# The residual x turned by VectorE in 32x32 blocks and kept in DRAM, instead of by TensorE in the out projection

## The chip, the cores and the metric

The kernel runs on one core of a Trainium2 chip. The metric is device time in microseconds, the median of several executions. TensorE (PE) multiplies, VectorE (DVE), ScalarE (ACT) and GpSimd (POOL) work elementwise, and SyncE (SP) issues most of the DMAs; each engine runs its own instructions in order, and semaphores tie them together.

## The reference

One decoder layer for 1024 prompt rows and 32 sample rows (8 sequences of 4), T = 1056 rows of D = 1024, all in fp32. Cut to what matters:

```python
def hybrid_layer(x, p, ...):
    h = rmsnorm(x, norm_mix)
    proj = h @ w_in                       # q, k, v, decay and beta, z, short conv b, c, h
    qkv = silu(causal_dwconv(qkv_in, w_conv_qkv))
    o, s_new = gated_delta_rule(q, k, v, log_a, beta, s0)   # 4 heads x 128, in chunks
    o = rmsnorm(o, w_gdn_norm) * silu(z)
    y_sc = B * causal_dwconv(C * h)       # the short convolution mixer
    x = x + concatenate([o, y_sc]) @ w_out    # the out projection, and its residual
    u = relu(rmsnorm(x, norm_mlp) @ w_up)
    x = x + (u * u) @ w_down
    x = x + sigmoid(rmsnorm(x, norm_ple) @ w_ple_gate) * (p @ w_ple_proj)
    return x, ...                          # then a last rmsnorm; conv rows and states are outputs too
```

## The kernel before, in words

Everything is kept transposed: features on the 128 partitions, the 1056 rows along the free axis, in three thirds of 352 (`TH`), one PSUM bank (`pg0` to `pg2`) each. Every product of fp32 numbers is made of three, from high and low parts: w_hi with act_hi, w_hi with act_lo, w_lo with act_hi. The work on TensorE is a row of units of 128 output features: a unit is 3 thirds of 24 matmuls (8 blocks of 128 input features, three products each).

For each unit SP loads 512 KB of weights into one of two buffers (`load_w`), ScalarE makes w_hi of them when TensorE has ended the unit before last (`split_w`, its line shows as L1164), VectorE makes w_lo (L1569), and only then may TensorE begin. VectorE takes each third out of PSUM; TensorE may begin third n of a unit when third n of the unit before is out (`group`, the wait on `evacuated`).

The order of stages: x is loaded in rows and turned by TensorE (L753), with a small product for the decays. Units 1 to 4 are k, 5 to 8 q (L695), 9 to 12 v, then z and the short convolution. During units 1 to 8 VectorE takes out the thirds (L1626, L1628), makes w_lo of the unit after next, then runs the causal convolution of the unit (L1646, L1649) and, in some units, a short chain of small operations for the decays; ScalarE makes SiLU of it. From unit 9 on, TensorE's matmuls are dealt out between the steps of the delta rule by a plan written out by hand (`ORDER`): a step name, chunk, level, and the number of matmuls of the units (L813) that follow. The plan's step `begin` on SP writes the decays as rows to DRAM (L589), waits until they have landed, reads them back twice (L570) and then loads the weights of units 10 and 11.

The out projection is 8 units (`out_unit`). The first takes the mix as soon as its parts are made (L1063), the low parts by VectorE (L1917) and POOL (L2310). The residual x is loaded from the input by SP, a block of 128 features of all rows at a time, into `x_col` (`load_xcol`); behind each third of products TensorE turns the matching pieces (3, 4 and 4 of them, L1041) into the banks `bk0` to `bk2`; ScalarE copies each third to `xres`, and VectorE adds the products (L2014). ScalarE squares each third for the next norm and POOL sums the squares. In the last unit ScalarE and VectorE also split each third of all of x into act_hi and act_lo (L2001) for the MLP, whose first unit waits for them third by third, with the sums of squares (L1075) behind its second third.

Of the kernel before, what the change touches and what calls it, by code (L numbers as in the profile page):

```python
# [105 lines left out]
class Signals:  # L106


    def __init__(self, sem):
# [71 lines left out]
        self.xcol_turned = sem("xcol_turned")  # L181
        self.xcol_turned3 = sem("xcol_turned3")
        self.xr_copied = sem("xr_copied")
# [60 lines left out]
def trunk(nc, x_p, x_s, st_qkv, st_gdn, st_sc, p_p, p_s, norm_mix, w_in, w_cq, a_log, dt_bias, w_gn, w_cs,  # L244
# [8 lines left out]
    g_dram = nc.dram_tensor("g_rows", (NTT * H, P), f32, kind="Internal").ap()  # L253
    y_dram = nc.dram_tensor("ysc_spill", (NSC * P, T), f32, kind="Internal").ap()
# [9 lines left out]
    with ctx:  # L264
# [31 lines left out]
        stage_x.close()  # L296
        qkv = sb("qkv", [P, NQ, T], scope=mixer)
# [69 lines left out]
        late = ExitStack()  # L367

        qkv_room = sb("qkv_room", [P, NQ, T], scope=late)
        x_col = [sb(f"x_col{i}", [P, NTT + 1, P], scope=late) for i in range(2)]  # L370
        late.close()
# [18 lines left out]
        xcol_in = [sem(f"xcol_in{i}") for i in range(2)]  # L390
        y_sent = [sem(f"y_sent{i}") for i in range(3)]
# [3 lines left out]


# [125 lines left out]
        def _(sp):  # L522
# [41 lines left out]
            for b in range(U_QKV + 2, U_V + 1):  # L564
                load_in(b)
# [6 lines left out]
            def load_xcol(x, i):  # L572
                f = ds(i * WIDE + x * P, P)
                sp.dma_start(x_col[x][:, 0:NTT, :], x_p[0].rearrange("(t p) d -> p t d", p=P)[:, :, f]) \
                    .then_inc(xcol_in[x], 16)
                sp.dma_start(x_col[x][0:TS, NTT, :], x_s.rearrange("b t d -> (b t) d")[:, f]) \
                    .then_inc(xcol_in[x], 16)
# [8 lines left out]
            for k, c, l, a, e in PLAN:  # L586
# [52 lines left out]
                if k == "sum" and c == NTT - 1:  # L639
                    load_y(1, slice(TP - 2 * P, T), NTT)  # L640
                    sp.wait_ge(sm.s_updated, 4 * NTT)
                    sp.dma_start(os_p[0, 0].rearrange("h d e -> d h e"), S[:, :, :]).then_inc(sm.states_out, 16)
                    for x in range(2):
                        load_xcol(x, 0)
# [7 lines left out]
            with sp.Fori(1, KD // 2) as i:  # L652
                for x in range(2):
                    load_w(U_OUT + x, i, wout_v[:, :, ds(i * WIDE + x * P, P)], KD)
                    sp.wait_ge(sm.xcol_turned, at(x - 1, i, 2))
                    load_xcol(x, i)
# [32 lines left out]
        def _(pe):  # L689
# [337 lines left out]
            for i in range(NSC):  # L1027
# [4 lines left out]
            pieces = [[(0, 0, 128, 0), (1, 0, 128, 128), (2, 0, 96, 256)],  # L1032
                      [(2, 96, 128, 0), (3, 0, 128, 32), (4, 0, 128, 160), (5, 0, 64, 288)],
                      [(5, 64, 128, 0), (6, 0, 128, 64), (7, 0, 128, 192), (8, 0, 32, 320)]]

            def turn_residual(x, i, n):

                pe.wait_ge(sm.consts_made, 3)
                pe.wait_ge(xcol_in[x], at(32, i, 32))
                for t, a, e, c in pieces[n]:  # L1040
                    last = turn(bk[n][:, c:c + e - a], x_col[x][a:e, t, :], ident[a:e, a:e])  # L1041
                last.then_inc(sm.xcol_turned if n == 2 else sm.xcol_turned3, 1)
# [11 lines left out]
            for n in range(3):  # L1054
# [11 lines left out]
                turn_residual(0, 0, n)  # L1066
# [95 lines left out]
        def _(act):  # L1162
# [59 lines left out]
            def silu_unit(b):  # L1222

                act.wait_ge(sm.conv_step, 4 * b)
# [194 lines left out]
            def out_pair(i):  # L1419
                last = isinstance(i, int)  # L1420
                for x in range(2):
                    b = U_OUT + x
                    def residual(n):

                        act.wait_ge(sm.xcol_turned if n == 2 else sm.xcol_turned3,
                                    at(x + 1, i, 2) if n == 2 else at(2 * x + n + 1, i, 4))
# [968 lines left out]
```

## Time and profile before

| | us |
|---|---|
| median of 3 runs | 1544.12 (1543.38 to 1544.9) |
| the profiled execution | 1544.85 |
| its span | 1542.9 |
| PE busy | 1496.4 (97%), 9412 matmuls |
| DVE busy | 726.8 (47%) |
| ACT busy | 483.8 (31%) |
| POOL busy | 248.5 (16%) |

Times in the rows are counted from the start of the span. "Busy" of PE is a modelled end of each matmul: one of 352 columns shows as 0.32 us while the next starts 0.16 us after it, so the pace is read from the starts. In a row of the timeline "x3" are three instructions merged; in brackets stands how long the engine sat idle before it, and what ended that. "issue" means that nothing in the profile shows what it waited for, which is often a DMA. The span's stages: x turned to 30 us, k and q units to 129, the mixer to 534, the out projection to 645, MLP to 1400, then the gated embedding and the last norm.

### The profile page before, as it was taken

The page shows a single profiled execution, that of the slowest core. Times are in us where ns is not written, and L with a number is a line of the kernel's source. Part 1 is how long each engine was busy: PE and PEld are TensorE (multiplying, and loading weights), DVE is VectorE, ACT ScalarE, POOL GpSimd, SP SyncE. Part 2 cuts the span into 40 slices and gives each one's busy share as a digit, 9 for nine tenths or more (in the row PEclk, how much of TensorE's full clock was granted, in tenths as well). Part 3 has the DMA queues.
Part 4 walks back from the last instruction along what each step waited for, and adds up shares of the span by engine and source line. Part 5 has one row for each costly group of instructions (what it writes and reads, how often), then busy time and mean ns, then how long its engine had stood idle before and what let it go on. Part 6 is the DMA issues. An engine that isn't in the chain of part 4 may idle for free.

```text
span 1542.9 us, 24976 instructions
## 1 busy us (share of the span) xinstructions
PE 1496.4 (97%) x9412; PEld 1458.7 (95%) x9412; DVE 726.8 (47%) x1305; ACT 483.8 (31%) x878; POOL 248.5 (16%) x306
## 2 busy tenths in 40 slices
PE   7998899899999999999999999999999999998997
PEld 6998898799999989899999999999999999998997
DVE  5666943377685632443433333333433433335525
ACT  6223432223333432543212131221302213136525
POOL 3200312043544542200000000000000000040303
PEclk9999997799999999999999999999999999999998
DMA  7212312312122223111111111111111111112102
GB/s 173 56 28 68 84 32 65 116 28 70 36 76 87 81 71 83 55 56 41 42 55 41 41 55 41 41 55 41 41 55 41 45 51 41 49 47 61 36 28 113
DMA packets 140204, 89.82 MB, mean 58 GB/s; under 512 B 16204, under 2 KB 134156, under 8 KB 140119
## 3 DMA queue, kind: packets, MB, share of 16 engines
q1 hardware_dynamic: 139110, 84.89, 19.2%
q0 software_dynamic: 1008, 3.79, 0.6%
q8 instruction: 55, 0.90, 0.3%
q14 instruction: 31, 0.25, 0.1%
HBM read 77.97 MB, written 10.69 MB: 57 GB/s over the span
## 4 chain that ended last, share of the span: by engine, by line
PE 89%; DVE 4%; issue 2%; POOL 2%; ACT 1%; DMA 0%; DVEq 0%; POOLq 0%; ACTq 0%; SPq 0%
PE pg L695 65%; PE pg L813 13%; PE bk L870 1%; DVE act_lo L2001 1%; PE bk L884 1%; PE bk L888 1%; PE bk L1041 1%; PE bk L840 1%; PE bk L1021 1%; POOL act_lo L2310 1%; PE bk L921 0%; DVE cv L1649 0%; PE bk L854 0%; PE bk L901 0%; PE bk L933 0%
## 5 line engine op out<-in xcount | busy, mean ns | idle before, releaser
L695 PE MATMUL pg<-act_hi,w_hi 128*128 128x352 f32 x1344 | 437.9, 326 | 12.5 <-issue 4.8
L695 PE MATMUL pg<-act_lo,w_hi 128*128 128x352 f32 x1344 | 431.8, 321 | 0.0
L695 PE MATMUL pg<-act_hi,w_lo 128*128 128x352 f32 x1320 | 423.2, 321 | 0.0
L695 PEld LDWEIGHTS pg<-act_hi,w_hi 128*128 128x128 f32 x1344 | 252.9, 188 | 16.4 <-issue 8.8
L695 PEld LDWEIGHTS pg<-act_lo,w_hi 128*128 128x128 f32 x1344 | 253.5, 189 | 0.0
L695 PE MATMUL pg<-u_hi,w_hi 128*128 128x352 f32 x768 | 249.3, 325 | 0.0
L695 PE MATMUL pg<-u_hi,w_lo 128*128 128x352 f32 x768 | 248.9, 324 | 0.0
L695 PE MATMUL pg<-u_lo,w_hi 128*128 128x352 f32 x768 | 247.8, 323 | 0.0
L695 PEld LDWEIGHTS pg<-act_hi,w_lo 128*128 128x128 f32 x1320 | 247.5, 188 | 0.0
L2351 POOL TENSOR_TENSOR ssq<-ssq,sq 128x352 f32<-128x352 f32 x72 | 78.1, 1098 | 892.4 <-ACT sq L1164 891.5
L1164 ACT ACTIVATE w_hi<-w_raw 128x1024 fp32r<-128x1024 f32 x111 | 117.1, 1055 | 333.8 <-PE pg L695 303.9
L2048 DVE TENSOR_TENSOR xres<-xres,pg 128x352 f32 (+1 forms) x192 | 99.2, 520 | 200.9 <-PE pg L695 200.9
L1569 DVE TENSOR_TENSOR w_lo<-w_raw,w_hi 128x1024 fp32r<-128x1024 f32 x110 | 141.9, 1290 | 69.0 <-ACT w_hi L1164 68.9
L813 PE MATMUL pg<-act_hi,w_hi 128*128 128x352 f32 x480 | 162.7, 339 | 2.9 <-DVE pre L1626 2.3
L813 PE MATMUL pg<-act_hi,w_lo 128*128 128x352 f32 x480 | 162.2, 338 | 0.0
L813 PE MATMUL pg<-act_lo,w_hi 128*128 128x352 f32 x480 | 160.4, 334 | 0.0
L695 PEld LDWEIGHTS pg<-u_hi,w_hi 128*128 128x128 f32 x768 | 145.0, 189 | 0.0
L695 PEld LDWEIGHTS pg<-u_lo,w_hi 128*128 128x128 f32 x768 | 144.5, 188 | 0.0
L695 PEld LDWEIGHTS pg<-u_hi,w_lo 128*128 128x128 f32 x768 | 143.9, 187 | 0.0
L1164 ACT ACTIVATE sq<-tm 128x352 f32<-128x352 f32 x96 | 48.0, 500 | 230.7 <-DVE tm L2034 230.7
L2038 DVE TENSOR_TENSOR u_lo<-sq,u_hi 128x352 f32 x96 | 50.5, 526 | 130.3 <-ACT u_hi L1164 130.3
L813 PEld LDWEIGHTS pg<-act_hi,w_hi 128*128 128x128 f32 x480 | 93.2, 194 | 8.8 <-issue 5.9
(333 smaller groups left out, 1685.3 us busy)
## 6 DMA issues: line engine op xcount, KB each, us to landing
w_raw<-in_w_up SPq DMA_DIRECT2D x32, 512.0 KB, 4.0
w_raw<-in_w_down SPq DMA_DIRECT2D x32, 512.0 KB, 3.4
w_raw<-in_w_in SPq DMA_DIRECT2D x29, 512.0 KB, 4.4
x_tok<-in_x_prompt SPq DMA_DIRECT2D x8, 512.0 KB, 7.3
w_raw<-in_w_out SPq DMA_DIRECT2D x8, 512.0 KB, 4.9
x_col<-in_x_prompt SPq DMA_DIRECT2D x8, 512.0 KB, 3.7
w_raw<-in_w_ple_gate SPq DMA_DIRECT2D x8, 512.0 KB, 4.0
out<-y_tok SPq DMA_DIRECT2D x8, 512.0 KB, 2.7
```

The lines of the kernel that those rows point to most:

```text
L695: last = mm(pg[bank][:, 0:TH], w, a, start=i == 0, stop=i == len(terms) - 1)
L813: last = mm(pg[n][:, 0:TH], w, (act_hi, act_lo, act_hi)[r][:, k, cols(n)], start=k == 0 and r == 0, stop=k == KD - 1 and r == 2)
L840: last = mm(bk[4][:, c:c + 8], S_in[:, h, i, :], F0[:, c:c + 8], start=True, stop=True)
L870: per_head(lambda h, v: mm(A[x][:, v], LY[x][:, h, :], X[x][:, h, :], start=True, stop=True)) \
L884: last = per_head(lambda h, v: mm(A[x][:, v], XT[s][x][:, h, :], LY[x][:, h, :], start=True, stop=True))
L888: last = per_head(lambda h, v: mm(bank[:, v], LY[x][:, h, :], XT[s][x][:, h, :], start=True, stop=True))
L1021: mm(bk[c % 4][:, :], F0[0:TS, c // 2 * P:(c // 2 + 1) * P], by_seq[c % 4][0:TS, :, :], start=True, stop=True).then_inc(sm.q_pe, 1)
L1164: return nc.scalar.activation(out, in_, func, **kw)
L1569: tt(w_lo[b % 2][:, :, :], w_raw[b % 2][:, :, :], w_hi[b % 2][:, :, :].bitcast(f32), SUB) \
L2038: tt(rows(u_lo[c % 2][:, k, cols(n)]), sq[g % 2][:, :], rows(u_hi[c % 2][:, k, cols(n)]).bitcast(f32), SUB).then_inc(sm.u_lo_made, 1)
L2048: tt(x_t, x_t, pg[g % 3][:, 0:TH], ADD).then_inc(sm.evacuated, 2)
L2351: tt(ssq[:, cols(n)], ssq[:, cols(n)], sq[g % 2][:, :], ADD).then_inc(sm.ssq_added, 1)
```

## The change

x for the residual is turned during units 1 to 8 and kept in DRAM in the transposed layout (`x_turned_rows`, 1024 x 1056). For each block j of 128 features SP loads x so that a partition holds a row of every 32 rows' block: four DMAs of 32 partitions (256 rows each, runs of 512 bytes). One VectorE instruction transposes all 32x32 blocks of a 128x1024 tile, and four DMAs store it in runs of 1 KB, which puts the blocks in their places. The 32 sample rows of all blocks go in one tile, with runs of 128 bytes both ways. The first loads wait until x has been squared, since their buffers lie over its room (and over that of q, k and v, not yet made).

VectorE does blocks 0, 1 and the samples behind unit 1's convolution, block j behind unit j's for 2 to 7. SP stores each and loads the block two further on, between its loads of weights; ScalarE waits for the last stores before SiLU of unit 8, whose room they use. In the out projection the 8 x 11 transposes of TensorE, ScalarE's copies and the `x_col` loads are gone: SP loads each block of the turned x into `xres` (528 KB), and VectorE's add waits for that DMA.

```diff
+            def load_x(j):
+                for a in range(4):
+                    src = x_p[0, 2 * P * a:2 * P * (a + 1), j * P:(j + 1) * P].rearrange("(q i) d -> i q d", i=32)
+                    sp.dma_start(x_col[j % 2][32 * a:32 * a + 32, :, :], src).then_inc(xcol_in[j % 2], 16)
+            def load_x_samples():
+                src = x_s.rearrange("s t (k b j) -> b (s t) k j", k=KD, b=4)
+                for b in range(4):
+                    sp.dma_start(x_smp[32 * b:32 * b + 32, :, :], src[b]).then_inc(xcol_in[0], 16)
+            def store_x(j):
+                dst = xt_dram[j * P:(j + 1) * P, 0:TP].rearrange("(b j) (a m) -> a j b m", b=4, a=4)
+                for a in range(4):
+                    sp.dma_start(dst[a], x_turn[j % 2][32 * a:32 * a + 32, :, :]).then_inc(xt_out[j % 2], 16)
+            sp.wait_ge(sm.st_turned, 1)
+            sp.wait_ge(sm.x_squared, NTT + 1)
+            load_x(0)
+            load_x_samples()
+            load_x(1)
+            for b in range(U_QKV + 2, U_V + 3):
+                if b < U_V + 1:
+                    load_in(b)
+                j = b - 4
+                if j == 1:
+                    sp.wait_ge(sm.x_blocked, 3)
+                    store_x(0)
+                    store_x(1)
+                    sp.dma_start(xt_dram.rearrange("(k p) t -> p k t", p=P)[:, :, TP:T], x_smp_turn[:, :, :]) \
+                        .then_inc(xt_out[0], 16)
+                    load_x(2)
+                    load_x(3)
+                elif j > 1:
+                    sp.wait_ge(sm.x_blocked, j + 2)
+                    store_x(j)
+                    if j + 2 < KD:
+                        load_x(j + 2)
@@ SP
+            def load_residual(j):
+                if j < 2:
+                    sp.wait_ge(xt_out[0], xt_count(KD - 2))
+                    sp.wait_ge(xt_out[1], xt_count(KD - 1))
+                else:
+                    sp.wait_ge(xcol_in[j % 2], xcol_count(KD - 2 + j % 2) + 16 * (j // 2))
+                sp.dma_start(xres[:, j, :], xt_dram[j * P:(j + 1) * P, :]).then_inc(xcol_in[j % 2], 16)
@@ SP, behind the plan
+            sp.wait_ge(sm.y_made, 3 * NSC)
+            sp.wait_ge(sm.state_saved, 2 * NQ + 2 * NSC)
+            sp.wait_ge(sm.op_mm, NTT)
+            load_residual(0)
+            load_residual(1)
@@ SP, the later units
-                    sp.wait_ge(sm.xcol_turned, at(x - 1, i, 2))
-                    load_xcol(x, i)
+                    load_residual(2 * i + x)
@@ PE
                     group(b, i, 4 * n, 4, n, parts(b % 2, KD, 0, act_hi, act_lo, n))
-                    turn_residual(x, i, n)
@@ ACT
             def silu_unit(b):
+                if b == U_V - 1:
+                    act.wait_ge(xt_out[0], xt_count(KD - 2))
+                    act.wait_ge(xt_out[1], xt_count(KD - 1))
@@ ACT, out_pair
-                    residual(0)
-                    residual(1)
-                    if not splits:
-                        residual(2)
@@ DVE
+            def x_blocks(j):
+                dve.wait_ge(xcol_in[j % 2], xcol_count(j))
+                if j >= 2:
+                    dve.wait_ge(xt_out[j % 2], xt_count(j - 2))
+                nc.vector.transpose(x_turn[j % 2][:, :, :], x_col[j % 2][:, :, :].rearrange("p q (b j) -> p b q j", b=4)) \
+                    .then_inc(sm.x_blocked, 1)
@@ DVE, units 1 to 8
                 convolve(b)
+                if b == 1:
+                    x_blocks(0)
+                    x_blocks(1)
+                    nc.vector.transpose(flat(x_smp_turn), flat(x_smp)).then_inc(sm.x_blocked, 1)
+                elif b < KD:
+                    x_blocks(b)
@@ DVE, out_pair
-                        dve.wait_ge(sm.xr_copied, at(3 * x + n + 1, i, 6))
+                        dve.wait_ge(xcol_in[x], at(xcol_count(KD - 2 + x) + 16, i, 16))
```

## Rows read from the trace of the kernel before

**Rows 1.** The chain that ended last, by engine (page, part 4).
```profile
PE 89%; DVE 4%; issue 2%; POOL 2%; ACT 1%; DMA 0%; DVEq 0%; POOLq 0%; ACTq 0%; SPq 0%
```

**Rows 2.** Timeline of PE, first products of two neighbouring thirds 0 (start us, us, engine, line).
```profile
563.82 0.43 PE L695 MATMUL pg<-act_hi,w_hi 128*128 128x352 f32 x1
...
577.50 0.43 PE L695 MATMUL pg<-act_hi,w_hi 128*128 128x352 f32 x1
```

**Rows 3.** The chain that ended last, in order of time: unit 8.
```profile
117.94 11.46 PE pg L695 x72
```

**Rows 4.** Timeline of PE, first out unit, third 2, and unit 1.
```profile
545.83 0.43 PE L1063 MATMUL pg<-act_hi,w_hi 128*128 128x352 f32 x1 [0.61 <-POOL act_lo L2310]
...
549.12 0.32 PE L1063 MATMUL pg<-act_hi,w_lo 128*128 128x352 f32 x1
...
550.17 0.40 PE L695 MATMUL pg<-act_hi,w_hi 128*128 128x352 f32 x1
```

**Rows 5.** Timeline of ACT, DVE and PE at the end of the out projection.
```profile
641.30 0.47 ACT L1164 ACTIVATE xres<-bk 128x352 f32<-128x352 f32 x1 [4.13 <-PE bk L1041]
...
642.05 3.96 ACT L1164 ACTIVATE act_hi<-xres,n_mlp 128x352 fp32r<-128x352 f32 x8
...
654.36 4.36 DVE L2001 SCALAR_TENSOR_TENSOR act_lo<-xres,n_mlp,act_hi 128x352 fp32r<-128x352 f32 x8 [1.05 <-ACT act_hi L1164]
...
644.96 0.32 PE L695 MATMUL pg<-act_hi,w_lo 128*128 128x352 f32 x1
...
652.93 0.43 PE L695 MATMUL pg<-act_hi,w_hi 128*128 128x352 f32 x1 [1.74 <-DVE act_lo L2001]
...
658.77 0.43 PE L695 MATMUL pg<-act_hi,w_hi 128*128 128x352 f32 x1
```

**Rows 6.** Stretches: us, busy of each engine, PEclk, DMA share, GB/s.
```profile
10.00:20.00 10.00, 6.91 (x31) 6.71 (x32) 8.27 (x13) 8.74 (x17) 4.57 (x5) 0.89 1.07 305
59.60:71.10 11.50, 11.50 (x74) 11.50 (x73) 8.20 (x13) 2.25 (x3) 0.54 (x3) 1.00 0.18 47
```

**Rows 7.** Timeline of DVE: take-outs of unit 2, thirds 0 and 1, then 2.
```profile
57.95 0.96 DVE L1626 TENSOR_TENSOR pre<-pg,r_b 128x352 f32<-128x352 f32 x2
59.70 0.49 DVE L1626 TENSOR_TENSOR pre<-pg,r_b 128x320 f32<-128x320 f32 x1 [0.80 <-PE pg L695]
```

**Rows 8.** DMA issues: count, KB each, median us to landing.
```profile
w_raw<-in_w_in SPq DMA_DIRECT2D x29, 512.0 KB, 4.4
...
z_spill<-cv POOLq DMA_DIRECT2D x4, 528.0 KB, 3.1
```

**Rows 9.** Groups by form: VectorE passes (busy us, mean ns, idle before).
```profile
L1569 DVE TENSOR_TENSOR w_lo<-w_raw,w_hi 128x1024 fp32r<-128x1024 f32 x110 | 141.9, 1290 | 69.0 <-ACT w_hi L1164 68.9
...
L1887 DVE STREAM_TRANSPOSE XT<-X 128x512 f32<-128x512 f32 x8 | 5.7, 711 | 0.3
...
L1848 DVE STREAM_TRANSPOSE X<-X 128x512 f32<-128x512 f32 x4 | 4.2, 1062 | 0.7 <-ACT X L1164 0.7
```

**Rows 10.** Timeline of DVE, SP, ACT and PE where the mixer begins.
```profile
120.91 4.10 DVE L1649 SCALAR_TENSOR_TENSOR cv<-pre,cq_w,cv 128x1080 f32<-128x1080 f32 x3
...
126.41 0.33 SPq L589 DMA_DIRECT2D g_rows<-LY  x1
...
128.68 22.88 SPq L528 DMA_DIRECT2D w_raw<-in_w_in  x4
...
134.67 1.06 ACT L1164 ACTIVATE w_hi<-w_raw 128x1024 fp32r<-128x1024 f32 x1 [8.29 <-issue]
...
142.40 0.40 PE L813 MATMUL pg<-act_hi,w_hi 128*128 128x352 f32 x1 [0.64 <-DVE pre L1626]
```

**Rows 11.** Timeline of PE behind two idle times, and a stretch's PEclk.
```profile
156.68 2.05 PE L862 MATMUL bk<-qkv 128*128 128x128 f32 x8 [6.20 <-DVE PT L1844]
...
170.83 0.43 PE L813 MATMUL pg<-act_hi,w_hi 128*128 128x352 f32 x1 [1.69 <-DVE pre L1626]
...
154.00:156.00 2.00, 0.00 (x0) 0.00 (x0) 1.78 (x10) 0.54 (x3) 0.00 (x0) 0.59 0.27 81
```

More of the change, by code:

```diff
@@ L180, in __init__ @@
         self.mix_hi = sem("mix_hi")
-        self.xcol_turned = sem("xcol_turned")
-        self.xcol_turned3 = sem("xcol_turned3")
-        self.xr_copied = sem("xr_copied")
+        self.x_blocked = sem("x_blocked")
         self.x_made = sem("x_made")
@@ L253, in trunk @@
     g_dram = nc.dram_tensor("g_rows", (NTT * H, P), f32, kind="Internal").ap()
+    xt_dram = nc.dram_tensor("x_turned_rows", (D, T), f32, kind="Internal").ap()
     y_dram = nc.dram_tensor("ysc_spill", (NSC * P, T), f32, kind="Internal").ap()
@@ L296, in trunk @@
         stage_x.close()
+        early = ExitStack()
+        k_q_room = sb("k_q_room", [P, 2 * H - 1, T], scope=early)
+        x_smp = sb("x_smp", [P, KD, TS], scope=early)
+        x_smp_turn = sb("x_smp_turn", [P, KD, TS], scope=early)
+        q_room = sb("q_room", [P, T - 2 * KD * TS], scope=early)
+        x_col = [sb(f"x_col{i}", [P, NTT, P], scope=early) for i in range(2)]
+        x_turn = [sb(f"x_turn{i}", [P, 4, 2 * P], scope=early) for i in range(2)]
+        early.close()
         qkv = sb("qkv", [P, NQ, T], scope=mixer)
@@ L366, in trunk @@
         tail.close()
[L367 to L371, printed above, removed]
         ple = ExitStack()
@@ L390, in trunk, with xcol_count, xt_count @@
         xcol_in = [sem(f"xcol_in{i}") for i in range(2)]
+        xt_out = [sem(f"xt_out{i}") for i in range(2)]
         y_sent = [sem(f"y_sent{i}") for i in range(3)]
         sm = Signals(sem)
+        def xcol_count(j):
+            return 64 * (j // 2 + 1) + 64 * (1 - j % 2)
+        def xt_count(j):
+            return 64 * (j // 2 + 1) + 16 * (1 - j % 2)
         def at(base, p=0, step=1):
@@ L642, in _ @@
                     sp.dma_start(os_p[0, 0].rearrange("h d e -> d h e"), S[:, :, :]).then_inc(sm.states_out, 16)
-                    for x in range(2):
-                        load_xcol(x, 0)
                 for b, n in thirds(a, e):
@@ L651, in _ @@
                 .then_inc(sm.states_out, 16)
-            with sp.Fori(1, KD // 2) as i:
+            for i in range(1, KD // 2):
                 for x in range(2):
-                    load_w(U_OUT + x, i, wout_v[:, :, ds(i * WIDE + x * P, P)], KD)
-                    sp.wait_ge(sm.xcol_turned, at(x - 1, i, 2))
-                    load_xcol(x, i)
+                    load_w(U_OUT + x, i, wout_v[:, :, i * WIDE + x * P:i * WIDE + (x + 1) * P], KD)
+                    load_residual(2 * i + x)
             for kind, c in MLP_ORDER:
@@ L1029, in _ @@
             last.then_inc(sm.so_turned, 1)
[L1032 to L1042, printed above, removed]
             def out_unit(x, i):
@@ L1065, in _ @@
                 last.then_inc(sm.mm_done, 4)
-                turn_residual(0, 0, n)
             out_unit(1, 0)
@@ L1422, in out_pair @@
                     b = U_OUT + x
-                    def residual(n):
-                        act.wait_ge(sm.xcol_turned if n == 2 else sm.xcol_turned3,
-                                    at(x + 1, i, 2) if n == 2 else at(2 * x + n + 1, i, 4))
-                        act.wait_ge(sm.consts_made, 3)
-                        op(xres[:, ds(2 * i + x, 1), cols(n)].rearrange("p a t -> p (a t)"), bk[n][:, 0:TH],
-                           ACT.Copy).then_inc(sm.xr_copied, 1)
                     splits = last and x == 1
-                    residual(0)
-                    residual(1)
-                    if not splits:
-                        residual(2)
                     act.wait_ge(sm.sample_states_out, 16 * H)
@@ L1449, in out_pair @@
                             split_x(n_mlp, n)
-                            if n == 0:
-                                residual(2)
             with act.Fori(0, KD // 2 - 1) as i:
```

8 lines of the change are left out of this document (removed).

## The prediction

> **What bounds the kernel now.** I first read the chain that ended last on the page: TensorE carries 89% of it, VectorE 4%, idle issue time 2% [rows 1]. So a cut on TensorE counts in full wherever TensorE is the engine that is late, and work added elsewhere costs nothing until TensorE waits for it. The question is which stretches that holds for. I then read four stretches of the timeline: the out projection in steady state, its beginning, its end, and the k and q units where the new work goes.
>
> In the out projection nothing but TensorE sets the pace. Third 0 of one unit starts at 563.82 and of the next at 577.50: 13.68 us for 72 products and 11 transposes [rows 2]. The same 72 products without transposes take 11.46 us in unit 8 [rows 3]. So the 11 transposes cost 13.68 - 11.46 = 2.2 us a unit, and no other engine is near that pace.
>
> The beginning is another matter. In the first out unit the products of third 2 wait for POOL's low parts of the mix: TensorE is idle 0.61 us before 545.83 [rows 4]. The transposes behind thirds 0 and 1 lie ahead of that wait, so taking them out gives nothing. Only those behind third 2 count: its last product starts at 549.12, ends its slot at 549.28, and unit 1 starts at 550.17.
>
> At the end there is more than the transposes. In the last unit ScalarE first copies the turned x of third 1 (641.30), which waits for TensorE's transposes behind third 1's products, and only then squares and splits third 0 (642.05) [rows 5]. From there the splits of three thirds run between ScalarE and VectorE at 5.85 us each. The first up unit waits for them: 1.74 us idle before 652.93, and third 2 starts at 658.77, when the last low part is done (654.36 + 4.36 = 658.72).
>
> In the k and q units TensorE is busy throughout. VectorE is busy 8.20 of 11.50 us in such a unit, the DMA engines 0.18 of the time [rows 6]. Unit 1 is fuller: a chain of small operations for the decay rates follows the convolution, and VectorE reaches unit 2's third 0 only at 57.95; unit 2 itself ends at 59.65 (its third 2 is taken out at 59.70) [rows 7]. TensorE may start unit 3 only when third 0 of unit 2 is out, so VectorE has about 59.65 - 58.45 = 1.2 us to spare.
>
> **The out projection: what is removed.** Unit 1 now starts at 549.28 instead of 550.17. Seven units of 11.5 us (between 11.46 and 11.56) end at 549.28 + 80.5 = 629.8, against 645.12 before (the last product starts at 644.96). That is 15.3 us. The last unit starts at S = 618.3; its third 0 is done at S + 3.8, VectorE's add ends at S + 4.4, the square at S + 4.85. The splits then begin there, against 642.05 - 632.3 = 9.7 after the start of the unit before: ScalarE no longer waits for transposes. The low part of third 2 is ready 658.72 - 642.05 = 16.7 later, at S + 21.5. TensorE has ended the unit at S + 11.5, third 0 of the up unit at S + 15.3, third 1 (ready at S + 15.7) at S + 19.6 and the sums at S + 21.4, so it starts third 2 at S + 21.6 = 639.9. Before it was 658.77: **18.9 us less**, 15.3 from the transposes and the rest from the earlier start of the splits. Everything behind hangs on that point and moves with it. Bounds by the unit's pace: 18.5 and 19.2.
>
> The residual's new path must not be late. It leaves SP when POOL has made the last product of the short convolution, one low part, 1.2 us, ahead of 545.83 [rows 4], so at about 544.6: two loads of 528 KB. By the spill of that size the first lands 3.1 us later, by the load of weights 4.4 [rows 8]; with VectorE's add of 0.5 the first unit's third 0 is out at 548.2 to 549.5. Unit 1 wants that bank at 549.28. So the cover is thin here: I take nothing, the bound is 0.3 us, or 1 if the two loads share the queue badly. Behind this wait on VectorE stand the unit's other adds and w_lo, which have a whole unit of time; the later residuals are loaded a unit ahead. ScalarE's 24 copies go as well; it had idle time, so they count for nothing except in the last unit.
>
> **The k and q units: what is added.** One transpose of 128x1024 in each of units 2 to 7, two in unit 1 and a small one of 128x256. The nearest rows are transposes of 512 elements: 711 ns flat, 1062 ns with a strided side [rows 9]. A VectorE pass over 128x1024 takes 1290 ns in the same rows. I take 1.23 us, because both innermost runs are contiguous here; the bounds are 0.7 (no more than the 512 one) and 2.0 (the strided one twice). The small one is 0.43. The Trainium skill, "VectorE: DVE Perf Modes", section "The TRN2 errata", gives (N + 151)/0.96 ns for an fp32 pass of two tensors: 1.22 us at 1024 and 0.69 at 512 as an estimate from the page. The row at 512 is near it.
>
> Unit 1: 2 x 1.23 + 0.43 = 2.9 us ahead of the take-out at 57.95. Third 0 of unit 2 is out at 61.35, TensorE starts unit 3 at 61.4 instead of 59.65: **+1.75 us**. Bounds: 0.5 with 0.7 each, 3.3 with 2.0 each; and up to 1.5 more (my margin, from no row) if the weights of unit 3 come late. Their load now stands on SP behind 12 loads of x, which wait until ScalarE has squared x; 1 MB of x takes some 9 us end to end and the weights 4.4 more [rows 8], so they land near the end of unit 1, where ScalarE wants them. The later units have 11.50 - 8.20 = 3.3 us to spare, so their transposes lie beside TensorE's work. DMA: a load of weights and one of x, 4.4 us each, and a store of 3.1 a unit [rows 8] are 11.9 us end to end, about a unit; but they overlap (305 GB/s were moved between 10 and 20 us, against 47 here) [rows 6], and each is wanted only a unit after its issue.
>
> The last store is the second cost. SP now waits for VectorE's transpose of unit 7 and issues four stores before it writes out the decay rows. VectorE's convolution ends at 125.0, the transpose then at 126.3, which is when SP wrote the rows anyway (126.41); four issues at 0.4 us (that of the rows took 0.33) are 1.6 us. The rows must land, be read back twice, and only then comes the load of unit 10's weights (128.68) [rows 10]. ScalarE splits these at 134.67 after 8.29 us idle, VectorE has to take the split, the convolution of unit 8 and the take-out, and TensorE stands 0.64 us before 142.40 for that. There is no slack: each us later at 128.68 is a us on the path. Behind the stores the rows' landing slows: at worst to the 3.1 us of a spill instead of some 1.4. I take 1.6 + 0.9 = **+2.5 us**; bounds 1.6 and 4.0 (1.6, 1.7 for the landing, 0.7 for a slower transpose). The Trainium skill, "DMA: Bandwidth & Descriptors", section "Queues, rings and completion order", says that a completion increment lands only after every earlier write of that DMA engine. By that the rows wait for the whole store and 1.6 + 1.7 = 3.3 us would be the likelier. No row of before shows the two together.
>
> ScalarE's new wait before unit 8's SiLU costs nothing: the stores it asks for are issued ahead of unit 10's weights, and this SiLU stands behind ScalarE's split of those. Behind the wait are the decays' exponentials, which VectorE needs next.
>
> **Sum.** -18.9 + 1.75 + 2.5 = -14.65 us. The profiled execution took 1544.85 (span 1542.9, 1.95 around it): 1530.2. The median of the runs is 0.73 lower, so I forecast 1529.5.
>
> **The rivals.** (a) The added work hides: transposes at 0.7 us and no delay behind the store but issue hidden too. Then only 0.5 of cost stays: 1525.7. For it: the 1.2 us of slack in unit 1; against: four issues on SP come ahead of a load with no slack. 0.10. (b) Costs at their upper ends, or TensorE's clock falls in the longer idle time. The idle before 142.40 grows from 0.64 to some 3 us. After 1.69 us idle before 170.83 the clock stayed at 1.00, in the 6.2 us idle before 156.68 it was 0.59 on the mean of 154 to 156, on its way from the level of 2.4 GHz to that of 1.2 GHz [rows 11]. With 3.3 us in unit 1 and 4.0 behind the store the gain is 11.6; with one stretch of some 7 us at the lower level (3.4 lost) it is 11.2: 1533. 0.20. (c) The splits don't start earlier, for another wait takes the copies' place (the residual's landing, the squares' sum): 15.3 - 4.25 = 11 saved, 1533.1. Against: these loads are issued a unit or more ahead. 0.10. (d) Slower: the blocked transpose streams far slower than its rows. It decides from 3.3 us each on, when VectorE fills a unit; then each of 6 units pays the excess and unit 1 twice. 2.5 + 2x - 0.7 + 6(x - 3.3) = 18.9 gives x = 4.6; with 5 us it is 1547. For it: the input is cut into four runs of 32 and no row has this shape; against: even the strided row would be 2.1. 0.04. (e) The projection doesn't get faster: each add waits for its residual from memory, which takes over the 2.2 us; the costs stay and eat up what the earlier splits give: about 1544.5. Against: the loads are issued a unit ahead of use. 0.03. My own case has 0.53, with 1527.5 to 1531.5.
>
> Range: (b) and (c) inside, (a) at the edge: 1525.5 to 1536. A change of 0.2%, 3.1 us, is about what a measurement can tell from none. Faster by more 0.93, within 0.03, slower 0.04.
>
> **What would show it.** Right: out units of 11.5 us with no products between but weights'; act_hi splits starting 4.9 us into the last unit; a TensorE idle of about 1.7 us near 59.7 with VectorE's take-out as its end; ScalarE's split of unit 10's weights 2.5 us later against the end of unit 8. Wrong: transposes above 2 us, idle for VectorE on the x loads, adds in the out projection idle on DMA, or a lower clock between 142 and 150.

## The result, and the profile after

The changed kernel took 1530.76 us in the median (1530.34 to 1531.45), the kernel before 1544.51 beside it. The ratio is 0.9912 with a 95% interval of 0.9895 to 0.993: 13.8 us faster, 0.9%. The forecast was 1529.5 us, in a range of 1525.5 to 1536.0. The profiled execution took 1530.34, its span is 1528.5, 14.4 less than the 1542.9 of before.

The out projection does what was forecast. The chain that ended last still belongs to TensorE (page, part 4, against [rows 1]):

```profile
PE 87%; DVE 6%; issue 3%; ACT 2%; POOL 2%; DMA 0%; SPq 0%; DVEq 0%; POOLq 0%
```

The timeline of VectorE shows the first adds of the out projection, then the adds of third 0 of two neighbouring units, then the last unit's, and the low parts behind it (start, us, engine, line):

```profile
554.77 0.95 DVE L2054 TENSOR_TENSOR xres<-xres,pg 128x352 f32 x2 [3.41 <-DMA xres<-x_turned_rows]
...
605.67 0.52 DVE L2054 TENSOR_TENSOR xres<-xres,pg 128x352 f32 x1 [1.57 <-PE pg L746]
...
616.97 0.52 DVE L2054 TENSOR_TENSOR xres<-xres,pg 128x352 f32<-128x352 f32 x1 [1.42 <-PE pg L746]
...
628.41 0.52 DVE L2054 TENSOR_TENSOR xres<-xres,pg 128x352 f32<-128x352 f32 x1 [1.55 <-PE pg L746]
630.03 4.36 DVE L2041 SCALAR_TENSOR_TENSOR act_lo<-xres,n_mlp,act_hi 128x352 fp32r<-128x352 f32 x8 [1.10 <-ACT act_hi L1201]
```

A unit is 11.3 to 11.4 us long, where it was 13.68 [rows 2], and there the adds wait for products, not for their residual; only the first one waited for memory. The low parts begin 1.6 us behind the last unit's first add. And TensorE takes up the first up unit's third 2 at 646.13, not at 658.77 [rows 5]. The first row below is TensorE's third 2 in the first out unit, where the forecast begins to count (545.83 before, [rows 4]): it comes 6.38 us later than before, and the last row 12.64 us sooner:

```profile
552.21 0.43 PE L1101 MATMUL pg<-act_hi,w_hi 128*128 128x352 f32 x1 [1.55 <-POOL act_lo L2350]
...
640.29 0.43 PE L746 MATMUL pg<-act_hi,w_hi 128*128 128x352 f32 x1 [0.52 <-DVE act_lo L2041]
644.21 1.94 PE L1112 MATMUL bk<-ssq,ones 128*128 128x352 f32 x6
646.13 0.43 PE L746 MATMUL pg<-act_hi,w_hi 128*128 128x352 f32 x1
```

The k and q units cost more than forecast. The timeline of VectorE and TensorE there, against [rows 7], and the stretches behind it (us, busy of each engine, PEclk, DMA share, GB/s):

```profile
57.67 2.36 DVE L1688 STREAM_TRANSPOSE x_turn<-x_col 128x1024 f32<-128x1024 f32 x2
59.96 0.40 DVE L1762 STREAM_TRANSPOSE x_smp_turn<-x_smp 128x256 f32<-128x256 f32 x1
...
61.61 1.35 DVE L1652 TENSOR_TENSOR pre<-pg,r_b 128x352 f32<-128x352 f32 x3
...
62.27 0.63 PE L746 MATMUL pg<-act_hi,w_hi 128*128 128x352 f32 x1 [2.80 <-DVE pre L1652]
...
60.00:62.00 2.00, 0.00 (x0) 0.00 (x0) 1.77 (x8) 0.57 (x1) 0.00 (x0) 0.97 0.33 75
62.00:64.00 2.00, 1.73 (x6) 1.75 (x7) 2.00 (x5) 0.00 (x0) 0.88 (x1) 0.50 0.96 257
64.00:66.00 2.00, 2.00 (x11) 2.00 (x10) 1.97 (x3) 0.00 (x0) 0.94 (x2) 0.68 0.96 218
```

The transposes cost what was forecast: 2.36 us for two, 1.24 for one alone, 0.40 for the samples. But TensorE stands 2.80 us, not 1.7, and behind it runs at the lower of its two levels: 0.50 is 1.2 GHz. Before, this stretch was at 1.00 throughout.

Where the mixer begins, timelines of SP, ScalarE and TensorE, against [rows 10]:

```profile
130.44 1.75 SPq L590 DMA_DIRECT2D x_turned_rows<-x_turn  x4
132.23 0.44 SPq L638 DMA_DIRECT2D g_rows<-LY  x1
134.24 0.82 SPq L618 DMA_DIRECT2D LY<-g_rows  x2
135.11 1.06 SPq L537 DMA_DIRECT2D w_raw<-in_w_in  x2
...
141.15 1.06 ACT L1201 ACTIVATE w_hi<-w_raw 128x1024 fp32r<-128x1024 f32 x1 [10.53 <-issue]
...
148.88 0.40 PE L864 MATMUL pg<-act_hi,w_hi 128*128 128x352 f32 x1 [2.87 <-DVE pre L1652]
```

The four stores stand ahead of the rows, and the rows land 2.01 us behind their issue (134.24 - 132.23) instead of 1.41 (127.82 - 126.41). The rest follows one for one: TensorE stands 2.87 us where it stood 0.64. Its clock stays up behind that idle time, although it is as long as the one before 62.27 (PEclk is the third number from the end):

```profile
148.00:150.00 2.00, 1.12 (x7) 1.16 (x8) 2.00 (x7) 1.57 (x3) 0.21 (x1) 1.00 0.00 0
150.00:152.00 2.00, 2.00 (x16) 2.00 (x15) 2.00 (x12) 1.99 (x3) 0.00 (x0) 1.00 0.03 8
```

To place all of it I measured five stretches between marks that every kernel here has: (a) from VectorE's take-out of third 2 of unit 1 to that of unit 8; (b) from there to the next such take-out in the mixer; (c) from there to the add of third 0 in the last out unit; (d) from there to the sums of squares; (e) the last norm, from VectorE's first scaled row to its last. In us, from one profiled execution of each:

| kernel | a | b | c | d | e |
|---|---|---|---|---|---|
| before | 81.17 | 17.96 | 489.92 | 19.55 | 14.64 |
| changed | 85.62 | 20.19 | 474.54 | 15.80 | 13.13 |
| changed_again | 86.23 | 20.08 | 473.95 | 15.86 | 14.61 |
| w3_first | 83.62 | 20.20 | 473.85 | 15.83 | 12.43 |
| x1_later | 83.74 | 20.22 | 474.28 | 15.85 | 13.32 |
| rows_first | 85.63 | 18.09 | 473.73 | 15.81 | 15.06 |
| all_three | 82.15 | 18.07 | 474.34 | 15.84 | 13.20 |
| spread_out | 81.50 | 18.10 | 473.82 | 15.80 | 12.99 |
| order_only | 81.18 | 18.00 | 487.59 | 20.03 | 12.99 |
| order_late | 81.34 | 18.02 | 487.58 | 16.40 | 14.68 |
| few_turns | 81.35 | 17.85 | 480.16 | 18.98 | 14.63 |
| two_each | 82.20 | 18.08 | 474.20 | 15.82 | 13.21 |
| four_each | 87.60 | 17.53 | 475.37 | 15.82 | 14.65 |

Between the two profiles of before and after: a + 4.45, b + 2.23, c and d together - 19.13, e - 1.51, the start, the MLP and the end - 0.44; together - 14.4, the difference of the spans.

### The profile page after: what moved, and what is told of

It reads as the page before. It is cut to its first block, busy times and chain, and to the rows that moved or that the text cites. A ratio compares the mean times of both kernels' runs of the same rounds, so it can differ in the third digit from the quotient of the medians.

```text
span 1528.5 us, 24745 instructions
## 1 busy us (share of the span) xinstructions
PE 1481.0 (97%) x9324; PEld 1451.0 (95%) x9324; DVE 733.6 (48%) x1314; ACT 473.9 (31%) x854; POOL 248.2 (16%) x306
## 4 chain that ended last, share of the span: by engine, by line
PE 87%; DVE 6%; issue 3%; ACT 2%; POOL 2%; DMA 0%; SPq 0%; DVEq 0%; POOLq 0%
PE pg L746 65%; PE pg L864 12%; PE bk L921 1%; DVE act_lo L2041 1%; PE bk L935 1%; PE bk L939 1%; PE bk L891 1%; PE bk L1072 1%; DVE cv L1675 1%; POOL act_lo L2350 1%; PE bk L1182 1%; DMA x_tok<-in_x_prompt 0%; ACT x_sqr L1201 0%; PE bk L905 0%; PE bk L984 0%
## 5 line engine op out<-in xcount | busy, mean ns | idle before, releaser
L746 PEld LDWEIGHTS pg<-act_hi,w_hi 128*128 128x128 f32 x1344 | 253.9, 189 | 14.8 <-issue 10.8
L864 PEld LDWEIGHTS pg<-act_hi,w_hi 128*128 128x128 f32 x480 | 93.3, 194 | 10.8 <-issue 8.1
```

What stands on the lines that cost most here:

```text
L746: last = mm(pg[bank][:, 0:TH], w, a, start=i == 0, stop=i == len(terms) - 1)
L864: last = mm(pg[n][:, 0:TH], w, (act_hi, act_lo, act_hi)[r][:, k, cols(n)], start=k == 0 and r == 0, stop=k == KD - 1 and r == 2)
```

## The experiments

Two theories stood against each other for the 4.45 us of stretch a, where 1.75 was forecast. Mine: three separate things in one place, namely the transposes on VectorE's path, unit 3's weights issued too late, and the lower clock behind a long idle time. The rival: the added traffic (15.0 MB written, not 10.7) or the transposes themselves slow this stretch wherever they stand.

**w3_first**, the changed kernel with unit 3's weights ahead of the loads of x:

```diff
+            load_in(U_QKV + 2)
             sp.wait_ge(sm.st_turned, 1)
             sp.wait_ge(sm.x_squared, NTT + 1)
...
-                if b < U_V + 1:
+                if U_QKV + 2 < b < U_V + 1:
                     load_in(b)
```

> The load of unit 3's weights is issued ahead of the 12 loads of x (28.4 us as before the change, not 43.7); all else as in the changed kernel. There TensorE stood 2.80 us before 62.27, and by 75 us it was 4.25 us behind the kernel before. My theory splits that 4.25 (with 0.2 gained ahead) into three: 1.75 of VectorE's transposes as predicted, 1.1 of late weights (VectorE's w_lo of unit 3 came at 50.43, not 49.35), and 1.5 of TensorE running at the lower clock (0.50 in 62 to 64 us, 0.68 in 64 to 66) behind the idle time. So here the idle is 1.7 us; if the clock then stays up, the mark is 1.6 us behind the kernel before and the time 1530.8 - 2.7 = 1528.1; if it falls all the same, 1529.7. Rival: the lateness is not the order of the issues but transposes waiting for x, or contention: then VectorE waits for x in unit 1, the idle stays at 2.8 and the time at 1530.8.

Its median was 1529.67. Stretch a is 83.62: 2.00 less than in the changed kernel, of 2.7 expected. The idle is 1.53 us, and the clock stays at 1.00:

```profile
62.10 0.40 PE L747 MATMUL pg<-act_hi,w_hi 128*128 128x352 f32 x1 [1.53 <-DVE pre L1653]
...
62.00:64.00 2.00, 1.90 (x12) 1.93 (x13) 2.00 (x5) 0.00 (x0) 1.06 (x1) 1.00 0.97 263
...
71.28 1.25 DVE L1689 STREAM_TRANSPOSE x_turn<-x_col 128x1024 f32<-128x1024 f32 x1 [2.44 <-DMA x_col<-in_x_prompt]
```

The last row shows why it is not 2.7: TensorE is sooner, so VectorE now comes to unit 2's transpose 2.44 us before block 2 of x has landed, and its take-out is late once more (TensorE idle 0.27 before 74.06). A part of the gain turned into a new wait. The second row speaks against the rival: the DMA engines are as busy (0.97 in 62 to 64) as in the changed kernel (0.96), and the clock is up.

**x1_later** instead moves the transposes:

```diff
                 if b == 1:
                     x_blocks(0)
+                elif b == 2:
                     x_blocks(1)
                     nc.vector.transpose(flat(x_smp_turn), flat(x_smp)).then_inc(sm.x_blocked, 1)
+                elif b == 3:
+                    x_blocks(2)
+                    x_blocks(3)
                 elif b < KD:
```

> VectorE transposes only block 0 in unit 1; block 1 and the samples in unit 2, blocks 2 and 3 in unit 3. Unit 3's weights stay late. Theory: TensorE's idle before 62.27 shrinks by 1.25 + 0.4 = 1.65 us, from 2.80 to 1.15, so the clock stays at 1.00 and 1.65 + 1.5 of the lower clock are saved: 1530.8 - 3.15 = 1527.6. The transposes in units 2 and 3 cost nothing, for VectorE had 3.3 us to spare in such a unit. Rival: the clock falls for another reason than the idle (the DMA share goes to 0.96 in the same slices), then only 1.65 is saved, 1529.1. Second rival: unit 3 with two transposes is too full, a new idle shows behind it and eats up 1 us or more.

The median was 1529.42; stretch a is 83.74, 1.9 less and not 3.15. The clock stays up there, as expected (it falls later, behind an idle time of 2.90 us before 147.80: 0.78 in 148 to 150 us, 0.50 in 150 to 152). But the idle is 1.70 us and not 1.15, for the weights came some 0.3 us later still, and unit 3 with its two transposes and a wait of 0.69 us for x costs another 0.6: the second rival, in small.

**rows_first** takes the decay rows past the last store:

```diff
-                elif j > 1:
+                elif 1 < j < KD - 1:
                     sp.wait_ge(sm.x_blocked, j + 2)
...
                     load_in(U_V + 1)
+                    sp.wait_ge(sm.x_blocked, KD + 1)
+                    store_x(KD - 1)
                     load_in(U_V + 2)
```

> SP writes the decay rows, reads them back and loads unit 10's weights before the store of block 7, not behind it. Theory: the write of the rows comes 1.57 us sooner (132.23 against 126.41 + 4.25) and lands in 1.4 us, not 2.0; both were on the path, so unit 10's split and all behind come 2.2 us sooner: 1528.6. ScalarE's wait for the stores before SiLU of unit 8 stays hidden, since the store is issued some 1 us behind the weights and lands before them. Rival: the slower landing is not of block 7's store but of other traffic, then 1.6 is saved (1529.2); or the store now slows the load of the weights, or ScalarE waits for it, then less than 1 (1530).

The median was 1529.54, stretch b 18.09 instead of 20.19: 2.1 us, of 2.2 expected. The rows land in 1.40 us (132.43 - 131.03) and ScalarE's split follows:

```profile
131.03 0.32 SPq L638 DMA_DIRECT2D g_rows<-LY  x1
132.43 0.82 SPq L618 DMA_DIRECT2D LY<-g_rows  x2
133.30 0.44 SPq L537 DMA_DIRECT2D w_raw<-in_w_in  x1
133.79 2.60 SPq L590 DMA_DIRECT2D x_turned_rows<-x_turn  x4
...
139.42 1.06 ACT L1203 ACTIVATE w_hi<-w_raw 128x1024 fp32r<-128x1024 f32 x1 [8.42 <-issue]
```

Stretch a has its idle (2.74 us) and lower clock here as in the changed kernel.

**all_three** joins the three edits.

> The three edits together: unit 3's weights first, block 1 and samples a unit later, decay rows before block 7's store. Theory: the costs ahead of the mixer vanish, 4.25 + 2.2 = 6.45 us: 1530.8 - 6.45 = 1524.3, with no TensorE idle over 0.3 us between 40 and 120 us and clock 1.00 there. Rival: the transposes or their 13 MB of traffic cost time wherever they stand (a shared limit, not a place on the path); then the three edits don't add up and the time stays above 1527.

Its median was 1526.32 (ratio 0.9886, 0.9871 to 0.9901): 4.4 us under the changed kernel, of 6.45 expected. Stretch b is back, a is at 82.15, 0.98 above before. What was left of a: VectorE's take-out in unit 2 came just too late (TensorE started unit 3 0.24 us late), and unit 3 had two transposes and a wait for x (unit 5 started 0.56 us late). **spread_out** is the same with no more than one in units 3 and 4. Against the changed kernel, the transposes now read:

```diff
-                if b == 1:
-                    x_blocks(0)
+                if b == 2:
                     x_blocks(1)
                     nc.vector.transpose(flat(x_smp_turn), flat(x_smp)).then_inc(sm.x_blocked, 1)
-                elif b < KD:
-                    x_blocks(b)
+                else:
+                    for j in {1: (0,), 3: (2,), 4: (3,), 5: (4, 5), 6: (6,), 7: (7,)}.get(b, ()):
+                        x_blocks(j)
```

> As the kernel with the three edits together, but no unit has two transposes of 128x1024 except unit 5, where no decay step follows: block 0 in unit 1, block 1 and samples in 2, block 2 in 3, block 3 in 4, blocks 4 and 5 in 5, then 6 and 7. With the three edits the stretch from the end of unit 1 to that of unit 8 was still 0.98 us longer than before the change; I put 0.65 of it down to two transposes and a wait of 0.73 us for x in unit 3. So here that stretch is 0.65 shorter than with the three edits (81.5 us against 82.15), and the time 0.65 lower. Rival: what is left is a cost of the DMA traffic, or of each transpose, and stays at 0.98.

It took 1524.42 us (1523.17 to 1525.91; ratio 0.9873, 0.9858 to 0.9888), 6.1 less than the changed kernel beside it, and stretch a is 81.50. So all the traffic and all nine transposes together cost 0.3 us there when they stand in the right places. This is the fastest kernel of the study.

**two_each** and **four_each** price the cover itself. In spread_out, blocks 2, 3 and 6 are transposed two or four times:

```diff
+                        for _ in range(3 if j in (2, 3, 6) else 0):
+                            turns_done[0] += 1
+                            turn_block(j).then_inc(sm.x_again, 1)
+                            dve.wait_ge(sm.x_again, turns_done[0])
                         x_blocks(j)
```

(`range(1 ...)` in two_each; `turn_block` is the transpose with its two waits.) Each of the two ran once; what follows is read from their traces.

> The kernel with the transposes spread out, with blocks 2, 3 and 6 (units 3, 4 and 6) transposed twice, 1.2 us more for VectorE in each. Theory (spare time on VectorE hides it): VectorE has the take-out of third 0 ready 1.8 us ahead of TensorE's need in unit 3 and about as much in unit 4, so the stretch from unit 1 to unit 8 stays at 81.5 us. Rival (TensorE pays for each transpose by some 0.3 us through a shared limit): it is 82.4.

> The same with the three blocks transposed four times each, 3.6 us more a unit. Now VectorE is late: third 0 is out at 81.8 + 3.6 = 85.4 in unit 3, TensorE wants it at 83.6, so 1.8 us of idle; 2.4 in unit 4 by the same rows; 0.8 in unit 6, where VectorE waited 1.9 us for ScalarE anyway. Theory: the stretch from unit 1 to unit 8 grows by 5.0 us to 86.5, and each idle stays under 2.7 us, so the clock holds. If idle times as short as 2.4 us already lower the clock, 88 us or more. Rival (nothing but DMA matters there): it stays under 83.

One more in each of the three units made a 0.70 us longer, between the two expectations. Only one unit started late: TensorE began unit 6 0.46 us late (at 95.33), behind unit 4's two transposes. Units 3 and 6 took their own for nothing; the other 0.24 lies in no single start. Three more made it 6.1 longer, of 5.0 expected: TensorE started unit 5 2.40 us late, unit 6 2.36 and unit 8 0.89 (each the distance of two starts less the pace of 0.16), and 0.4 is left over. The rows of four_each for the middle one, and the stretches:

```profile
97.22 0.32 PE L750 MATMUL pg<-act_hi,w_lo 128*128 128x352 f32 x1
99.74 0.40 PE L750 MATMUL pg<-act_hi,w_hi 128*128 128x352 f32 x1 [2.19 <-DVE pre L1656]
...
98.00:100.00 2.00, 0.26 (x2) 0.29 (x3) 1.81 (x7) 0.64 (x1) 0.00 (x0) 1.00 0.70 160
100.00:102.00 2.00, 2.00 (x14) 2.00 (x14) 2.00 (x5) 0.00 (x0) 1.42 (x2) 1.00 0.83 228
```

In unit 3 VectorE came to the take-out 3.84 us later than in spread_out (85.18, not 81.34) and TensorE lost 2.40 of it: 1.4 were to spare, which is why two_each cost nothing there. In unit 4 some 0.8 to 0.9 were. So work on VectorE is free up to the take-out's spare time and costs its full length beyond, and here the clock holds through 2.19 us of idle. The 2.7 us of the expectation is no limit, though: the changed kernel itself holds its clock behind 2.87 us (above).

The other question was what the 19.1 us of c and d consist of: 15.3 of transposes and 3.6 of splits that start sooner, by the forecast. **order_only** is the kernel before with only ScalarE's order changed in the last out unit:

```diff
                     residual(0)
-                    residual(1)
                     if not splits:
+                        residual(1)
                         residual(2)
...
                             if n == 0:
+                                residual(1)
                                 residual(2)
```

> The kernel before, with one thing moved: in the last out unit ScalarE copies the turned x of third 1 behind the splits of third 0, not ahead of them. All 88 transposes stay on TensorE. My theory is that the out projection's 19 us consist of 15.3 of transposes and 3.6 of splits that start sooner. Here the splits start 5.2 us into the last unit (third 0 with its transposes 4.4, VectorE's add, the square) instead of 9.7; TensorE then sets the pace (13.7 for the unit, three thirds of 3.85 to 4.1 with the sums): its third 2 of the first up unit starts 23.2 us behind the start of the last out unit, not 26.5. Gain 3.3 us against the kernel before. Rival: ScalarE and VectorE are too full there, so that the copies and splits only change places: gain under 0.5.

It took 1543.3 us (ratio 0.9994, 0.9985 to 1.0003): no difference that the runs can tell. Stretch d is 20.03, even 0.48 longer than before. I had not followed ScalarE's queue to its end. Its timeline:

```profile
636.12 0.50 ACT L1164 ACTIVATE sq<-xres 128x352 f32<-128x352 f32 x1 [0.74 <-DVE xres L2015]
...
644.27 0.46 ACT L1164 ACTIVATE xres<-bk 128x352 f32<-128x352 f32 x1 [3.46 <-PE bk L1041]
```

The copy of third 2, which waits for the transposes behind third 2's products, stood ahead of the square and the splits of third 1. The other part is chance: behind an idle time of 1.78 us TensorE's clock fell in this profile, and third 1's products of the up unit with it took 5.49 us (650.06 to 655.55) instead of 3.93:

```profile
650.06 0.43 PE L695 MATMUL pg<-act_hi,w_hi 128*128 128x352 f32 x1 [1.78 <-DVE act_lo L2002]
...
650.00:655.00 5.00, 4.94 (x21) 4.95 (x22) 3.96 (x9) 4.34 (x9) 0.94 (x1) 0.66 0.00 0
```

Without that, d would be some 18.5 and the gain 1.1, still not 3.3. **order_late** leaves third 1's copy where order_only has it, behind the splits of third 0, and puts third 2's behind those of third 1:

```diff
-                    residual(1)
                     if not splits:
+                        residual(1)
                         residual(2)
...
-                            if n == 0:
-                                residual(2)
+                            if n < 2:
+                                residual(n + 1)
```

> The kernel before again, with ScalarE's copies in the last out unit each put right ahead of its use: third 1's behind the splits of third 0, third 2's behind the splits of third 1. In the run with third 1's and third 2's both behind the splits of third 0, the copy of third 2 waited 3.46 us for TensorE's transposes and held up ScalarE's square and splits of third 1, so that only 1.85 us were gained and not 3.3. Theory: now the splits of third 1 begin 11.2 us into the unit, those of third 2 at 17.0, TensorE sets the pace, and the stretch from the mixer's first take-out to the up unit's sums is 3.3 us shorter than in the kernel before (506.2 against 509.47 us). Rival: the splits have less in them than I say; the stretch stays at 507.6.

Now the last unit's stretch d is 16.40 instead of 19.55, 3.15 less, and the time 1540.88 (ratio 0.9981, 0.9971 to 0.9992), 2.9 under before. The mark that the expectation named, b's end to the sums, fell by 5.5 (from 509.47 to 503.98), since it takes in stretch c, which is 2.3 shorter in order_only too; the 1.85 us that the expectation calls order_only's gain were a part of those 2.3, and these lie in the mixer, which no edit touched (below). The change of order alone is thus worth 3 us without any transpose gone.

**few_turns** is the other part: 3 of the 11 transposes of a unit are left, so its residual is incomplete.

```diff
-                for t, a, e, c in pieces[n]:
+                for t, a, e, c in pieces[n][:1]:
```

> The kernel before, with 3 of the 11 transposes of each out unit left (one behind each third) and 8 left out, so the residual is incomplete; loads, ScalarE's copies and their order stay. Theory: TensorE's pace falls by what the 8 take, 1.6 of 2.2 us a unit, so seven units save 11.2; ScalarE's copy of third 1 still waits for third 1 of the last unit, which comes 1.2 us sooner within the unit. Together 12 us, the stretch from the first out unit to the up unit's sums 99 us long instead of 111.0. Rival: the order of ScalarE's work follows by itself once TensorE is faster, then 3 more are saved, 96 us.

It took 1534.71 us (ratio 0.9938, 0.9924 to 0.9951), 9.6 less of some 12 expected. A unit is 12.35 us long; the 8 transposes took 1.33 of the 2.2 us, the three that are left 0.9. My share by count was wrong, since a part of the cost belongs to each change from products to transposes and back: in before, the product ahead of a group of transposes keeps TensorE up to 0.25 us and the one behind it 0.25 to 0.27, where the pace is 0.16. This profile also lost some 1.6 us to the clock in the first out unit (last section). Stretch d was 0.6 shorter, not 3.75: the splits did not come by themselves.

**changed_again** is the changed kernel beside these.

> The changed kernel once more, beside the others, as their measure. Theory: TensorE's idle before some 62 us is 2.7 to 2.8 us again, with the clock at its lower level behind it, and the stretch from unit 1 to unit 8 is 85.6 us as in the first profile. The last norm, which was 1.5 us shorter than in the kernel before (13.1 against 14.6 us between its first and last scaled rows), comes out anywhere between the two: I hold that for the clock of that stretch and not for the change. Rival: the shorter last norm is a part of the change, then it is 13.1 again.

It took 1530.55 (ratio 0.9912, 0.9899 to 0.9926). The idle was 3.24 us, longer than I expected, and stretch a 86.23, with the lower clock again (0.80, 0.50 and 0.84 from 62 to 68 us). The last norm was 14.61 us, as long as before the change; over all kernels it lies between 12.43 and 15.06, with and without the change. So the 1.5 us in the first pair of profiles are no part of it. The stretches of before and after show the clock in that place:

```profile
1530.00:1535.00 5.00, 4.43 (x22) 4.44 (x23) 2.01 (x4) 2.02 (x5) 0.00 (x0) 0.50 0.69 276
...
1535.00:1540.00 5.00, 4.05 (x28) 3.48 (x26) 2.91 (x4) 2.73 (x4) 0.00 (x0) 0.82 0.59 240
```

```profile
1517.00:1522.00 5.00, 4.51 (x30) 4.51 (x31) 2.68 (x5) 2.63 (x6) 0.00 (x0) 0.74 0.76 307
1522.00:1527.00 5.00, 2.73 (x20) 2.18 (x18) 2.24 (x3) 2.06 (x3) 0.00 (x0) 0.92 0.80 319
```

## Why the prediction was right, point by point

**The out projection, 18.9 us.** Right. The forecast counts from third 2 of the first out unit to third 2 of the first up unit. That took 112.94 us before (545.83 to 658.77) and takes 93.92 now (552.21 to 646.13): 19.02 less. order_late takes 109.37 (544.15 to 653.52), so 3.57 of the 19.02 belong to the order of ScalarE's work (3.6 forecast) and 15.45 to the transposes (15.3 forecast). Stretch c is no measure of it by itself, for it takes in the mixer: from b's end to that first mark before took 398.44 us, the changed kernel 398.34, order_only and order_late 396.1. These 2.3 us are in both profiles of before and after and fall out of their difference; the mean clock of 150 to 320 us was 0.86 in these two and 0.87 in the other two. One reserve is left: in four of the nine profiles with the change the clock falls in the first out unit, and the stretch is 1.6 us longer. Then the gain is 17.4. The last square and the splits begin where the forecast put them (the splits at 629.42, 4.8 us behind the take-out that ended the unit before, 624.60). The residual from memory was as close as forecast: VectorE waited 3.41 us for it before the first add at 554.77, and took third 0 out 0.4 us before TensorE began unit 1 at 555.65.

**The transposes, 1.23 and 0.43 us.** Right: 1.24 and 0.40. The Trainium skill, "VectorE: DVE Perf Modes", section "The TRN2 errata", gives a formula for fp32 passes of two tensors; an estimate from it is 1.22 us at 1024 elements and 0.42 at 256. The trace agrees (1.24 and 0.40), although these are transposes and their input is cut into runs of 32.

**Unit 1, 1.75 us.** The step that failed. The idle was 2.80 and stretch a grew by 4.45 (5.06 the second time). The stall was named, with its place and its cause; two things were kept for the range and not added. The late weights were there as "up to 1.5 more" and took 1.1 of it (VectorE's w_lo of unit 3 at 50.43, not 49.35). And the lower clock, priced in rival (b), did come, but in another place than (b) looked for it: behind 2.80 us of idle in the k units, while behind the 2.87 us where (b) expected it, where the mixer begins, it stayed at 1.00. w3_first and x1_later each took away the clock's share and about half of the idle, and spread_out brought a to within 0.3 us of before.

**Behind the last store, 2.5 us.** Right in size, 2.23 and 2.12: the issues took 1.6 us as forecast (rows 1.57 later than the shift ahead of them explains), the landing 0.6, not 0.9. The Trainium skill, "DMA: Bandwidth & Descriptors", section "Queues, rings and completion order", says that a completion lands only after all earlier writes of that DMA engine. The trace agrees: the last of the four stores was issued near 131.8 and such a store takes 2.3 us in the median, so by this estimate it landed near 134.1, and the rows were there at 134.2. My price for this rule was too high, for I took the landing of a 528 KB spill and not of 128 KB.

**The spare time of the later units, 3.3 us.** Too generous. It was worked out from VectorE's busy time in a unit. The spare time that counts is how far ahead of TensorE's need the take-out of third 0 comes, and two_each shows less than 1.2 us of it in unit 4 (four_each: 1.4 in unit 3).

**The sum.** - 18.9 + 1.75 + 2.5 came out as - 19.1 + 4.45 + 2.2 - 1.95 for the rest, of which 1.5 are the last norm's luck. So the forecast hit (1529.5 for 1530.76) with one term 2.7 us too small and a random gain of about the same size at the other end. By stages alone the change is worth 12.3 us (19.0 - 4.45 - 2.23), or 10.2 where the clock falls in the first out unit and stretch a is as long as the second time (17.4 - 5.06 - 2.12); the runs say 13.8 with an interval of 10.8 to 16.2. I can't tell these apart any finer.

**The rivals.** (a) is out: both costs were there. (b) was half right, as told: the costs were above my sum and a stretch ran at the lower clock. (c) is out: the splits started where forecast. (d) and (e) are out: a transpose took 1.24 us, and only the first add waited for DMA, with no product late for it.

## What to carry to other kernels

Ask of work moved to an idle engine not how busy that engine is but how long before the busy one needs its next hand-over it comes there; up to that the work is free, beyond it counts in full. A load or store put ahead of another on one queue delays it by every issue (0.4 us each) and, here, by the 0.6 us that its own landing took longer, so look at what is queued behind with no slack; here two moves of a few lines on SP and one on VectorE gave 6 us on top of 13.8. And where an engine's work is taken out, look at what waited for it on other engines: 3 to 3.6 of the 19 us came from two copies at the wrong places in ScalarE's queue, and were to be had without the change; moving only the first of them gained some 1.1 at best.

## What the runs showed of the hardware

- How long TensorE stood idle does not settle by itself whether its clock falls. In the k and q units the clock held behind 1.53, 1.70, 2.19 and 2.24 us and fell behind 2.74, 2.80 and 3.24 us. But where the mixer begins it held behind 2.75 (changed_again), 2.87 (changed) and 2.88 us (w3_first) and fell behind 2.90 (x1_later). In the last out unit it held behind 1.74 us (before) and fell behind 1.78 (order_only). And one idle time of 2.26 us, near 1380 us, stands in all 13 profiles: the clock fell behind it in five (0.88 on the mean of 1376 to 1390) and held in eight.
- At the lower level the same products started every 0.29 us instead of 0.16. Where the clock fell in the k units, 1.6 to 1.9 us were lost beside the idle itself.
- Where the clock is down is not the same from run to run, even for one program. In the first out unit, where TensorE without transposes stands 1.55 us (1.18 in few_turns) instead of 0.6 for POOL's low parts, the mean clock of 540 to 560 us was 0.91 in changed_again, w3_first, spread_out, four_each and few_turns and 1.00 in changed, x1_later, rows_first, all_three and two_each. The price is 1.6 us; in the kernels with all transposes I saw no such fall there. The mixer takes 2 us more in before and changed (mean clock of 150 to 320 us 0.86) than in order_only, order_late or changed_again (0.87), and the last norm differs by 2.6 between profiles. Gains of 1 or 2 us must be read from a stretch of the trace; the medians of w3_first, x1_later and rows_first, 1.1 to 1.3 us under the changed kernel, don't show what their stretches do.
- Transposes between products cost by their change-over too: of 11 in three places, which took 2.2 us a unit, the three that were left in few_turns, one in each place, still took 0.9.
